# Side work of ScalarE and VectorE in the head rounds of a two-layer transformer block, put in another order

## The chip, the cores and the metric

The kernel runs on one core of a Trainium2 chip. The time is the device time of one execution in microseconds. TensorE (PE) multiplies, VectorE (DVE), ScalarE (ACT) and GpSimd (POOL) work on rows of 128 partitions, SyncE (SP) issues most transfers. Each engine takes its instructions in the order in which they are written; the engines wait for each other through semaphores.

## The reference

Two layers over 256 context and 256 latent tokens (512 columns here, feature on the partitions): feed-forward half, token mixer, feed-forward half. The head rounds are the gated delta rule of the token mixer, eight heads of width 128, in both directions:

```python
def _dn_inputs(p, dn_conv):
    y = jax.nn.silu(_dwconv(p[6], dn_conv))            # three taps over time
    q, k, v = [t.reshape(B, T, DN_HEADS, DN_DIM) for t in jnp.split(y, 3, axis=-1)]
    return (_l2norm(q), _l2norm(k), v) + ...

def _gated_delta_chunked(q, k, v, g, beta, s0):
    ...
    decay_mat = jnp.where(incl, jnp.exp(jnp.where(incl, diff, 0.0)), 0.0)
    a_mat = jnp.where(strict, einsum(kb, kc) * decay_mat, 0.0)
    sol = lax.linalg.triangular_solve(a_mat, rhs, left_side=True, lower=True, unit_diagonal=True)
    attn_intra = einsum(qc, kc) * decay_mat
    def step(s, inp):
        v_new = u_i - w_i @ s
        o = (q_i * exp(g_i)) @ s + a_i @ v_new
        s = s * exp(g_last) + (k_i * exp(g_last - g_i)) ^T @ v_new
```

Its output is normed, gated with silu of a fourth projection, and goes on to the branch products. In layer 1 only the 256 latent columns of q, the gate and the output are wanted.

## The kernel before

**Weights.** All weight matrices come as one stream of panels of 128 x 1024, four to a block B. A panel goes through `raw` (four slots), is split by ScalarE into a high part `whi` (`split`, L479, counted by `hi_ready`) and by VectorE into the low part `wlo` (`split`, L976, waits for `hi_ready`, counted by `lo_ready`), and TensorE multiplies it in 24 matmuls (L1569), 8 tiles by three products. SP loads the next panel into a slot when its low part is made.

**Head rounds.** `heads(l)` walks over the eight heads of a layer: the first head is prepared, then come seven rounds that finish head b - 1 and prepare head b (`head(l, b, True)`; six of them a loop, the seventh written out), and a last one that only finishes (`head(l, DNH, False)`). A round works on the panels of block B (panels 2 and 3) and of block B + 1 (panels 0 and 1) between its own products, so that TensorE has matmuls while others work. I write (B,3) for panel 3 of block B. A following round goes:

1. *Half levels.* The inverse of the triangular matrix is built in seven levels v for two directions d; half level h = 2v + d runs from 0 to 13. TensorE does eight 128x128 products (L1804, L1806) and then three panel matmuls. Its result is copied by ScalarE (L727, "copy h") and masked by VectorE (L1278, "mask h"); both are read by half level h + 2. The copies of half levels 12 and 13 are L730, the subtractions L1293 of VectorE stand in the place of masks. Panel (B,2) fills the half levels 0 to 7, (B,3) those from 8 on. Behind half level 11 and behind half level 13 stands a square sum of TensorE (L1889).
2. *Rest of the inverse*, L1830 to L1303.
3. *Scan*, four steps s over chunks: TensorE L1847, L1857, L1865, L1875, L1877, VectorE L1310, L1316, L1320, L1329 and L1332 between them.
4. *Front and output* (`output_and_front`): output norm of head b - 1 (L696, L1250, L487, L489, L1261, L1267, L712) and the first matrices of head b (L1759, L1253, `low_a` L1230, L1778, `first_level` L1236 and L1239).

**Side work.** Between the copies ScalarE does, for head b: bias `prep_in` (L626), first tap `prep_tap` (L639), request of the gathered decay rows `load_rows` (L644, an own transfer), `prep_silu` (L655, and L659 the squares), for head b - 1 the gate's Silu (L743, with a table load), and its halves of four splits. Between the masks VectorE does the other two taps `prep_conv` (L1178, L1180), its halves of the splits, and `decay` (L1211 and four L1216), which needs the gathered rows. A tap of VectorE waits for the tap of ScalarE, a split of VectorE for that of ScalarE; everything behind it in VectorE's queue waits too. The place of each piece of side work is written by hand, as conditions on (v, d).

## Time and profile before

| | us |
|---|---|
| median of 3 runs | 3571.32 |
| lowest, highest | 3563.38, 3581.49 |
| the profiled execution | 3567.69 |
| its span, first to last instruction | 3565.9 |
| TensorE busy | 3297.0 (92%) |
| VectorE busy | 1736.1 (49%) |
| ScalarE busy | 1418.2 (40%) |

The head rounds are 548 to 1047 us and 2535 to 3008 us of the span. The profile page gives busy time by engine and the chain that ended last. The windows view gives the busy time of each engine in stretches, and the granted TensorE clock as a share of full speed: 1.00 is 2.4 GHz, 0.50 is 1.2 GHz. The timeline has one row per instruction or run of alike ones, in brackets the idle time of the engine before it and what ended it.

### The profile page before, as it was taken

The numbers are of one execution on the slowest core, as the hardware profiler recorded it, in microseconds if no ns is written. First come the engines' busy times: TensorE is split into PE (matmuls) and PEld (weight loads), VectorE is DVE, ScalarE is ACT, GpSimd is POOL, SyncE is SP. The second block draws the span as 40 slices with busy tenths as digits, with TensorE's granted clock in tenths as the row PEclk, the third lists the DMA queues.
The fourth block names the chain that finished last, engine by engine and source line by source line (L and its number), as shares of the span: only waits on it lengthen the run. The fifth ranks groups of instructions, "written<-read, shape, count | busy, mean of one in ns | idle before, by whom it ended". The sixth has DMA issues, their size and how long they took to land.

```text
span 3565.9 us, 51673 instructions
## 1 busy us (share of the span) xinstructions
PE 3297.0 (92%) x18878; PEld 2729.3 (77%) x18878; DVE 1736.1 (49%) x3152; ACT 1418.2 (40%) x2197; POOL 131.5 (4%) x126
## 2 busy tenths in 40 slices
PE   5999989999989899999999999999798888999898
PEld 3778767777768667877788877777687777789898
DVE  2333346666643753434333433334566665666555
ACT  3222244545433642224322342223454544564544
POOL 0000001001000000000000000000000000000000
PEclk7999979998999999999999999998899989999999
DMA  6444421111112124222423243442111111324454
GB/s 227 159 142 141 153 77 43 46 35 48 40 40 90 42 72 148 94 89 96 165 95 100 100 153 136 154 146 95 54 47 41 47 42 52 120 96 166 152 183 148
DMA packets 101117, 363.43 MB, mean 102 GB/s; under 512 B 11136, under 2 KB 12672, under 8 KB 100864
## 3 DMA queue, kind: packets, MB, share of 16 engines
q1 hardware_dynamic: 98240, 353.00, 29.2%
q10 hardware_dynamic: 2752, 8.72, 0.7%
q8 instruction: 84, 1.38, 0.2%
q14 instruction: 41, 0.34, 0.0%
HBM read 360.56 MB, written 1.11 MB: 101 GB/s over the span
## 4 chain that ended last, share of the span: by engine, by line
PE 79%; DVE 9%; ACT 6%; issue 4%; DMA 1%; POOL 0%; DVEq 0%; SPq 0%; ACTq 0%; POOLq 0%
PE bank L1569 62%; PE bank L1804 2%; PE bank L1806 2%; ACT whi L479 2%; DVE wlo L976 2%; PE bank L1594 2%; PE bank L1857 1%; DVE scr_r L1278 1%; PE bank L1889 1%; PE bank L1700 1%; PE bank L1830 1%; ACT scr L896 1%; DVE h L1043 1%; PE bank L2000 1%; DVE scr L1320 1%
## 5 line engine op out<-in xcount | busy, mean ns | idle before, releaser
L1569 PE MATMUL bank<-uh,whi 128*128 128x512 f32 (+1 forms) x3008 | 1125.3, 374 | 46.3 <-ACTq L854 15.0
L1569 PE MATMUL bank<-ul,whi 128*128 128x512 f32 (+1 forms) x3008 | 1092.5, 363 | 0.0
L1569 PE MATMUL bank<-uh,wlo 128*128 128x512 f32 (+1 forms) x3008 | 1091.0, 363 | 0.5 <-DVE scr L1320 0.3
L976 DVE TENSOR_TENSOR wlo<-raw,whi 128x1024 fp32r<-128x1024 f32 x520 | 642.5, 1236 | 877.9 <-ACT whi L479 876.1
L479 ACT ACTIVATE whi<-raw 128x1024 fp32r<-128x1024 f32 x520 | 547.6, 1055 | 1224.4 <-PE bank L1569 1224.0
L1569 PEld LDWEIGHTS bank<-uh,whi 128*128 128x128 f32 x3008 | 584.1, 194 | 149.0 <-issue 56.3
L1569 PEld LDWEIGHTS bank<-uh,wlo 128*128 128x128 f32 x3008 | 582.9, 194 | 83.5 <-DVE scr L1320 1.8
L1569 PEld LDWEIGHTS bank<-ul,whi 128*128 128x128 f32 x3008 | 584.3, 194 | 70.4 <-issue 1.7
L1569 PE MATMUL bank<-bh,whi 128*128 128x512 f32 (+1 forms) x1088 | 387.9, 357 | 1.1 <-DVE h L1043 0.8
L1569 PE MATMUL bank<-bl,whi 128*128 128x512 f32 (+1 forms) x1088 | 384.5, 353 | 0.0
L1569 PE MATMUL bank<-bh,wlo 128*128 128x512 f32 (+1 forms) x1088 | 384.4, 353 | 0.0
L1569 PEld LDWEIGHTS bank<-bh,whi 128*128 128x128 f32 x1088 | 205.8, 189 | 33.5 <-issue 4.3
L1804 PEld LDWEIGHTS bank<-scr_r 128*128 128x128 f32 x896 | 142.5, 209 | 113.6 <-issue 73.8
L1569 PEld LDWEIGHTS bank<-bl,whi 128*128 128x128 f32 x1088 | 205.8, 189 | 28.7 <-issue 1.0
L1569 PEld LDWEIGHTS bank<-bh,wlo 128*128 128x128 f32 x1088 | 205.8, 189 | 28.4
L1804 PE MATMUL bank<-scr_r 128*128 128x128 f32 x896 | 154.0, 298 | 63.2 <-DVE scr_r L1278 63.2
L1079 DVE TENSOR_TENSOR scr<-scr,bank 128x512 f32<-128x512 f32 (+1 forms) x88 | 54.6, 620 | 256.9 <-PE bank L1569 256.5
L727 ACT ACTIVATE scr_r<-bank 128x512 fp32r<-128x512 f32 x192 | 114.5, 596 | 131.8 <-PE bank L1806 130.2
L1806 PE MATMUL bank<-scr_r 128*128 128x128 f32 x896 | 151.0, 295 | 0.0
L1278 DVE TENSOR_TENSOR scr_r<-bank,cst 128x512 fp32r<-128x512 f32 x192 | 128.5, 685 | 43.3 <-PE bank L1806 43.3
L440 POOL TENSOR_TENSOR scr<-scr 128x512 f32<-128x512 f32 (+1 forms) x42 | 47.4, 1129 | 2375.2 <-ACT scr L513 2374.2
L1806 PEld LDWEIGHTS bank<-scr_r 128*128 128x128 f32 x896 | 132.3, 212 | 0.0
(231 smaller groups left out, 3149.0 us busy)
## 6 DMA issues: line engine op xcount, KB each, us to landing
raw<-stream SPq DMA_DIRECT2D x520, 512.0 KB, 3.3
ada_raw<-stream SPq DMA_DIRECT2D x132, 512.0 KB, 5.2
gc_row<-gc_rows ACTq DMA_DIRECT2D x16, 512.0 KB, 3.7
m<-stream SPq DMA_DIRECT2D x8, 512.0 KB, 11.5
scr<-stream SPq DMA_DIRECT2D x4, 512.0 KB, 13.1
h<-h_in SPq DMA_DIRECT2D x1, 2048.0 KB, 17.6
cst<-consts SPq DMA_DIRECT2D x1, 1282.0 KB, 5.6
out<-m SPq DMA_DIRECT2D x8, 128.0 KB, 1.8
```

The source lines that it names most:

```text
L440: pool.tensor_tensor(nacc[:, c0:T], nacc[:, c0:T], nsq[:, t % 2, c0:T], ALU.add).then_inc(sq_added, 1)
L479: act.activation(whi[:, j, :], raw[:, j, :], ACT.Copy).then_inc(hi_ready, 1)
L727: act.activation(XT[:, d, :], bank[4 + d][:, :], ACT.Copy).then_inc(E["qtr_ready"], 1)
L896: last = act.activation(Pb[:, n % 2, a, q * w:(q + 1) * w], bank[2 + 2 * (n % 2) + a][:, q * w:(q + 1) * w], ACT.Exp, scale=HD ** -0.5, bi ...
L976: dve.tensor_tensor(wlo[:, j, :], raw[:, j, :], whi[:, j, :].bitcast(f32), ALU.subtract).then_inc(lo_ready, 1)
L1043: last = stt(out=h[:, t, a:b], in0=bank[j][:, a:b], scalar=hgate[:, t, k:k + 1], in1=h[:, t, a:b], op0=ALU.mult, op1=ALU.add)
L1079: dve.tensor_tensor(hbuf[:, k, c0:T], sil[:, k, c0:T], bank[2 * k + 1][:, c0:T], ALU.mult).then_inc(pair_done[k], 1)
L1278: dve.tensor_tensor(c4d(Pm[:, d, :]), c4d(bank[7 - d][:, :]), mask, ALU.mult).then_inc(E["pm_ready"], 1)
L1569: last = mm(bank[j][:, c0:T], w(t, a), x[:, t, c0:T], start=n == 0, stop=n == 3 * kts - 1)
L1594: last = mm(bank[4][at:at + 32, 0:256], cstat[:, 2 * j + kk, :], w[:, 512 * kk + 256 * half:512 * kk + 256 * half + 256], start=j == 0, st ...
L1804: mm(qt[:, sl(c)], Pm[:, d, sl(c)], x[:, d, sl(c)], start=v == 0 and c == 0, stop=False, skip_group_check=True)
L1806: last = mm(q[:, sl(c)], x[:, d, sl(c)], Pm[:, d, sl(c)], start=v == 0 and c == 0, stop=False, skip_group_check=True)
```

## The change

The side work in the head rounds is put in another order. No instruction is added or removed.

- ScalarE: gate Silu from behind copy 5 to behind copy 6, `prep_silu(0)` from 6 to 7, first half of split (B+1,0) from 7 to 8, `prep_silu(1)` from 8 to 10, split (B+1,1) from 10 to 11, split (B+1,2) from behind `prep_silu(2)` to behind the copy of half level 12. The third bias and tap stay behind copy 9.
- VectorE: `prep_conv(1)` from behind mask 4 to 5, split (B,3) from 3 to 6, `decay(0)` from behind the two L1293 to behind mask 8, split (B+1,0) from 6 to 9, `prep_conv(2)` from 8 to 11, split (B+1,1) from 9 to between the two L1293, `decay(1)` from scan step 0 to behind the two L1293, split (B+1,2) from scan step 1 into `output_and_front`: ahead of the first `first_level`, and in a last round between the two output products.

The core of the diff:

```diff
@@ scalar, head()
-                        if (v, d) == (2, 1):
+                        if at == 6:
                             have(act, E["head_ready"], o)
                             act.activation(gate[:, c0:T], gpre[:, c0:T], ACT.Silu)
-                        if follow and (v, d) == (3, 0):
+                        if follow and at == 7:
                             prep_silu(l, b, 0)
-                        if (v, d) == (3, 1):
+                        if at == 8:
                             split(B + 1, 0)
-                        if follow and (v, d) == (4, 0):
-                            prep_silu(l, b, 1)
-                        if follow and (v, d) == (4, 1):
+                        if follow and at == 9:
                             prep_in(l, b, 2)
                             prep_tap(l, b, 2)
-                        if (v, d) == (5, 0):
+                        if follow and at == 10:
+                            prep_silu(l, b, 1)
+                        if at == 11:
                             split(B + 1, 1)
+                        if at == 12:
+                            split(B + 1, 2)
                 if follow:
                     prep_silu(l, b, 2)
-                split(B + 1, 2)
@@ vector, output_and_front()
                     low_a(1)
+                    if output:
+                        split(P[("head", l)][0] + b + 1, 2)
                     first_level(0)
...
+                elif output:
+                    split(P[("head", l)][0] + b + 1, 2)
@@ vector, head()
-                        if (v, d) == (2, 1):
+                        if follow and at == 5:
+                            prep_conv(l, b, 1)
+                        if at == 6:
                             split(B, 3)
-                        if follow and (v, d) == (3, 0):
-                            prep_conv(l, b, 1)
-                        if (v, d) == (4, 0):
+                        if follow and at == 8:
+                            decay(l, b, 0)
+                        if at == 9:
                             split(B + 1, 0)
-                        if follow and (v, d) == (5, 0):
+                        if follow and at == 11:
                             prep_conv(l, b, 2)
-                        if (v, d) == (5, 1):
-                            split(B + 1, 1)
...
+                    if d == 0:
+                        split(B + 1, 1)
                 if follow:
-                    decay(l, b, 0)
+                    decay(l, b, 1)
...
-                    if follow and s == 0:
-                        decay(l, b, 1)
...
-                    if s == 1:
-                        split(B + 1, 2)
```

**VectorE in the half levels** of the seventh round of layer 0 (written out in the code), from masks 0 to 2 on. L1278 is a mask, L976 a split, L1178 and L1180 a pair of taps. Before:

```order
404 L1278 TENSOR_TENSOR scr_r<-bank,cst 128x512 [waits q_sum] x3
405 L1178 SCALAR_TENSOR_TENSOR kraw<-scr,hv,kraw 128x512 [waits tap_ready,hv_ready]
406 L1180 SCALAR_TENSOR_TENSOR kraw<-scr,hv,kraw 128x512 [waits dve_step]
407 L1278 TENSOR_TENSOR scr_r<-bank,cst 128x512 [waits q_sum]
408 L976 TENSOR_TENSOR wlo<-raw,whi 128x1024 [waits hi_ready]
409 L1278 TENSOR_TENSOR scr_r<-bank,cst 128x512 [waits q_sum]
410 L1178 SCALAR_TENSOR_TENSOR scr<-scr,hv 128x512 [waits tap_ready,hv_ready]
411 L1180 SCALAR_TENSOR_TENSOR scr<-scr,hv 128x512 [waits dve_step]
412 L1278 TENSOR_TENSOR scr_r<-bank,cst 128x512 [waits q_sum] x2
413 L976 TENSOR_TENSOR wlo<-raw,whi 128x1024 [waits hi_ready]
```

After (the mask is L1284, the taps L1180 and L1182, the split L978, the decay L1213 and L1218):

```order
404 L1284 TENSOR_TENSOR scr_r<-bank,cst 128x512 [waits q_sum] x3
405 L1180 SCALAR_TENSOR_TENSOR kraw<-scr,hv,kraw 128x512 [waits tap_ready,hv_ready]
406 L1182 SCALAR_TENSOR_TENSOR kraw<-scr,hv,kraw 128x512 [waits dve_step]
407 L1284 TENSOR_TENSOR scr_r<-bank,cst 128x512 [waits q_sum] x3
408 L1180 SCALAR_TENSOR_TENSOR scr<-scr,hv 128x512 [waits tap_ready,hv_ready]
409 L1182 SCALAR_TENSOR_TENSOR scr<-scr,hv 128x512 [waits dve_step]
410 L1284 TENSOR_TENSOR scr_r<-bank,cst 128x512 [waits q_sum]
411 L978 TENSOR_TENSOR wlo<-raw,whi 128x1024 [waits hi_ready]
412 L1284 TENSOR_TENSOR scr_r<-bank,cst 128x512 [waits q_sum] x2
413 L1213 COPY hgc<-tab 128x8 [waits dm_ready]
414 L1218 SCALAR_TENSOR_TENSOR m<-gc_row,hgc,cst 128x128 [waits it_ready,gcr_loaded,hgc_ready]
415 L1218 SCALAR_TENSOR_TENSOR m<-gc_row,hgc,cst 128x128 x3
```

The split of (B,3) moved from behind mask 3 to behind mask 6, the second pair of taps from behind mask 4 to behind mask 5, and the first decay came in behind mask 8.

**ScalarE in the half levels** of the same round, from its half of split (B,3) on. L727 is a copy, L479 a split, L743 the gate, L655 and L659 Silu and squares, L626 and L639 bias and tap. Before:

```order
313 L479 ACTIVATE whi<-raw 128x1024 [waits panel_done,raw_in3]
314 L727 ACTIVATE scr_r<-bank 128x512 [waits q_sum]
315 L743 ACT_TABLE_LOAD
316 L743 ACTIVATE scr<-gate_pre 128x512 [waits head_ready]
317 L727 ACTIVATE scr_r<-bank 128x512 [waits q_sum]
318 L655 ACTIVATE kraw<-kraw 128x512 [waits conv_ready]
319 L659 ACTIVATE scr<-kraw 128x512 [waits it_ready,silu_ready]
320 L727 ACTIVATE scr_r<-bank 128x512 [waits q_sum]
321 L479 ACTIVATE whi<-raw 128x1024 [waits panel_done,raw_in0]
322 L727 ACTIVATE scr_r<-bank 128x512 [waits q_sum]
323 L655 ACTIVATE scr<-scr 128x512 [waits conv_ready]
324 L659 ACTIVATE scr<-scr 128x512 [waits it_ready,silu_ready]
```

After (the gate is L744):

```order
313 L479 ACTIVATE whi<-raw 128x1024 [waits panel_done,raw_in3]
314 L727 ACTIVATE scr_r<-bank 128x512 [waits q_sum] x2
315 L744 ACT_TABLE_LOAD
316 L744 ACTIVATE scr<-gate_pre 128x512 [waits head_ready]
317 L727 ACTIVATE scr_r<-bank 128x512 [waits q_sum]
318 L655 ACTIVATE kraw<-kraw 128x512 [waits conv_ready]
319 L659 ACTIVATE scr<-kraw 128x512 [waits it_ready,silu_ready]
320 L727 ACTIVATE scr_r<-bank 128x512 [waits q_sum]
321 L479 ACTIVATE whi<-raw 128x1024 [waits panel_done,raw_in0]
322 L727 ACTIVATE scr_r<-bank 128x512 [waits q_sum]
323 L626 ACTIVATE scr<-bank,hv 128x2x256 [waits panel_done,hv_ready]
324 L639 ACTIVATE scr<-scr,hv 128x512 [waits pre_ready]
```

The split of (B,3) stays where it was; everything from the gate on stands one copy later, and the third bias and tap come ahead of the second Silu.

**VectorE in the scan** of the same round, steps 0 and 1. Before:

```order
431 L1320 TENSOR_SCALAR scr<-bank,hb 128x128 x2
432 L1216 SCALAR_TENSOR_TENSOR m<-gc_row,hgc,cst 128x128 x4
433 L1329 COPY scr<-bank 128x128 [waits ds_sum] x2
434 L1310 SCALAR_TENSOR_TENSOR scr<-bank,hb,scr 128x128 [waits ks_sum] x2
435 L1316 TENSOR_SCALAR scr<-bank,hb 128x128 [waits y_sum] x2
436 L1320 TENSOR_SCALAR scr<-bank,hb 128x128 x2
437 L1332 SCALAR_TENSOR_TENSOR scr<-scr,hb,bank 128x128 [waits s_ready,ds_sum] x2
438 L976 TENSOR_TENSOR wlo<-raw,whi 128x1024 [waits hi_ready]
439 L1310 SCALAR_TENSOR_TENSOR scr<-bank,hb,scr 128x128 [waits ks_sum] x2
```

After:

```order
432 L1329 TENSOR_SCALAR scr<-bank,hb 128x128 x2
433 L1336 COPY scr<-bank 128x128 [waits ds_sum] x2
434 L1319 SCALAR_TENSOR_TENSOR scr<-bank,hb,scr 128x128 [waits ks_sum] x2
435 L1325 TENSOR_SCALAR scr<-bank,hb 128x128 [waits y_sum] x2
436 L1329 TENSOR_SCALAR scr<-bank,hb 128x128 x2
437 L1339 SCALAR_TENSOR_TENSOR scr<-scr,hb,bank 128x128 [waits s_ready,ds_sum] x2
438 L1319 SCALAR_TENSOR_TENSOR scr<-bank,hb,scr 128x128 [waits ks_sum] x2
```

The four instructions of the second decay left step 0 and the split left step 1.

## Rows read from the trace of the kernel before

**Rows 1.** Page, the chain that ended last

```profile
PE 79%; DVE 9%; ACT 6%; issue 4%; DMA 1%; POOL 0%; DVEq 0%; SPq 0%; ACTq 0%; POOLq 0%
```

**Rows 2.** Windows: half levels, rests of layer 0, of layer 1; last round

```profile
sum 210.50, PE 185.37 PEld 152.28 DVE 122.81 ACT 132.19 POOL 43.09; mean PE 26.48 PEld 21.75 DVE 17.54 ACT 18.88 POOL 6.16
...
sum 232.80, PE 223.93 PEld 184.34 DVE 166.66 ACT 92.69 POOL 0.00; mean PE 31.99 PEld 26.33 DVE 23.81 ACT 13.24 POOL 0.00
...
sum 203.80, PE 172.72 PEld 152.00 DVE 110.49 ACT 121.28 POOL 21.07; mean PE 24.67 PEld 21.71 DVE 15.78 ACT 17.33 POOL 3.01
...
sum 212.90, PE 192.59 PEld 165.98 DVE 160.24 ACT 81.04 POOL 0.00; mean PE 27.51 PEld 23.71 DVE 22.89 ACT 11.58 POOL 0.00
...
991.80:1017.00 25.20, 21.73 (x147) 18.94 (x145) 12.44 (x17) 13.16 (x19) 6.27 (x5) 1.00 0.19 61
```

**Rows 3.** Timeline (start, us, operation), round at 738.4: masks, taps, splits

```profile
742.65 0.69 DVE L1278 TENSOR_TENSOR scr_r<-bank,cst 128x512 fp32r<-128x512 f32 x1 [0.89 <-PE bank L1806]
...
744.13 1.66 DVE L1180 SCALAR_TENSOR_TENSOR kraw<-scr,hv,kraw 128x512 f32<-128x512 f32 x1
...
744.78 0.56 PE L1804 MATMUL bank<-scr_r 128*128 128x128 f32 x4
...
747.40 1.23 DVE L976 TENSOR_TENSOR wlo<-raw,whi 128x1024 fp32r<-128x1024 f32 x1 [1.01 <-ACT whi L479]
...
759.18 0.75 DVE L1178 SCALAR_TENSOR_TENSOR scr<-scr,hv 128x512 f32<-128x512 f32 x1 [2.64 <-ACT scr L639]
```

**Rows 4.** Timeline, a square sum of TensorE, and ScalarE in the round at 738.4

```profile
707.02 1.02 PE L1889 MATMUL bank<-scr,cst 128*128 128x512 f32 x2
...
746.31 1.05 ACT L479 ACTIVATE whi<-raw 128x1024 fp32r<-128x1024 f32 x1
...
748.28 1.28 ACT L743 ACT_TABLE_LOAD   x1
...
751.64 0.63 ACT L659 ACTIVATE scr<-kraw 128x512 f32<-128x512 f32 x1
752.55 0.60 ACT L727 ACTIVATE scr_r<-bank 128x512 fp32r<-128x512 f32 x1 [0.27 <-PE bank L1806]
...
758.43 0.72 ACT L639 ACTIVATE scr<-scr,hv 128x512 f32<-128x512 f32 x1
```

**Rows 5.** Waits of the seven layer 0 rounds (waited for, us, times, longest)

```profile
PE bank L1804 <- DVE scr_r L1278: 25.1, 26, 1.9
DVE wlo L976 <- ACT whi L479: 25.1, 15, 3.1
```

**Rows 6.** Windows: length, busy by engine (PE, PEld, DVE, ACT, POOL), clock

```profile
759.10:762.50 3.40, 1.47 (x11) 1.05 (x10) 3.28 (x5) 1.48 (x3) 0.00 (x0) 0.99 0.00 0
762.50:765.90 3.40, 3.40 (x9) 2.08 (x9) 1.15 (x2) 0.60 (x1) 0.00 (x0) 0.50 0.49 154
776.00:786.00 10.00, 9.37 (x64) 7.92 (x62) 8.04 (x27) 2.67 (x5) 0.00 (x0) 1.00 0.15 52
```

**Rows 7.** Timeline, scan: weight loads in layer 0 and 1, a decay of VectorE

```profile
715.93 0.52 PEld L1847 LDWEIGHTS bank<-scr 128*128 128x128 f32 x4 [0.84 <-DVE scr L1329]
...
2753.36 0.52 PEld L1847 LDWEIGHTS bank<-scr 128*128 128x128 f32 x4 [1.06 <-DVE scr L1329]
...
2757.91 0.55 PEld L1857 LDWEIGHTS bank<-scr,xtf 128*128 128x128 f32 x4 [0.99 <-DVE scr L1310]
...
2751.97 1.13 DVE L1216 SCALAR_TENSOR_TENSOR m<-gc_row,hgc,cst 128x128 f32<-128x128 f32 x4
```

**Rows 8.** Timeline, front: first transposed level of VectorE, layer 0 and 1

```profile
734.49 0.69 DVE L1236 TENSOR_TENSOR lmat<-bank,cst 128x512 f32<-128x512 f32 x1 [2.08 <-PE bank L1778]
...
2769.80 0.69 DVE L1236 TENSOR_TENSOR lmat<-bank,cst 128x512 f32<-128x512 f32 x1 [0.96 <-PE bank L1778]
```

**Rows 9.** Timeline, TensorE behind the last round of layer 0

```profile
1046.88 0.79 PE L1569 MATMUL bank<-uh,whi 128*128 128x512 f32 x1 [8.47 <-ACTq L854]
```

**Rows 10.** Gathered decay rows: transfer from issue to landing

```profile
DMA to landing us min/median/max: 3.4/3.7/4.3
```

More of the change, by code:

```diff
@@ L730, in head @@
                             act.activation(X[:, d, :], bank[7 - d][:, :], ACT.Copy, scale=-1.0).then_inc(E["x_ready"], 1)
-                        if follow and (v, d) == (0, 1):
+                        at = 2 * v + d
+                        if follow and at == 1:
                             prep_in(l, b, 0)
                             prep_tap(l, b, 0)
-                        if follow and (v, d) == (1, 0):
+                        if follow and at == 2:
                             prep_in(l, b, 1)
-                        if follow and (v, d) == (1, 1):
+                        if follow and at == 3:
                             load_rows(l, b)
                             prep_tap(l, b, 1)
-                        if (v, d) == (2, 0):
+                        if at == 4:
                             split(B, 3)
-                        if (v, d) == (2, 1):
+                        if at == 6:
                             have(act, E["head_ready"], o)
                             act.activation(gate[:, c0:T], gpre[:, c0:T], ACT.Silu)
-                        if follow and (v, d) == (3, 0):
+                        if follow and at == 7:
                             prep_silu(l, b, 0)
-                        if (v, d) == (3, 1):
+                        if at == 8:
                             split(B + 1, 0)
-                        if follow and (v, d) == (4, 0):
-                            prep_silu(l, b, 1)
-                        if follow and (v, d) == (4, 1):
+                        if follow and at == 9:
                             prep_in(l, b, 2)
                             prep_tap(l, b, 2)
-                        if (v, d) == (5, 0):
+                        if follow and at == 10:
+                            prep_silu(l, b, 1)
+                        if at == 11:
                             split(B + 1, 1)
+                        if at == 12:
+                            split(B + 1, 2)
                 if follow:
                     prep_silu(l, b, 2)
-                split(B + 1, 2)
                 log_exp()
@@ L1278, in head @@
                         dve.tensor_tensor(c4d(Pm[:, d, :]), c4d(bank[7 - d][:, :]), mask, ALU.mult).then_inc(E["pm_ready"], 1)
-                        if follow and (v, d) == (2, 0):
+                        at = 2 * (v - 1) + d
+                        if follow and at == 2:
                             prep_conv(l, b, 0)
-                        if (v, d) == (2, 1):
+                        if follow and at == 5:
+                            prep_conv(l, b, 1)
+                        if at == 6:
                             split(B, 3)
-                        if follow and (v, d) == (3, 0):
-                            prep_conv(l, b, 1)
-                        if (v, d) == (4, 0):
+                        if follow and at == 8:
+                            decay(l, b, 0)
+                        if at == 9:
                             split(B + 1, 0)
-                        if follow and (v, d) == (5, 0):
+                        if follow and at == 11:
                             prep_conv(l, b, 2)
-                        if (v, d) == (5, 1):
-                            split(B + 1, 1)
                 for d in range(2):
```

## The prediction, with its working

> **What bounds the kernel now.** I read the page first: the chain that ended last is TensorE for 79% of the span [rows 1], so time goes where TensorE stands still. The diff touches only the head rounds, so next come the windows of those rounds. There are 16: seven of layer 0 that also prepare the next head (the "following" rounds), seven of layer 1, and one last round in each layer. I cut each round at the start of its half level 13, the last of the fourteen half levels; a half level is one level of the inversion for one direction, with three panel matmuls behind it. The sum rows say: 210.5 us in the seven stretches of half levels of layer 0 (30.07 a round) and 232.8 us in their rests (33.26), 203.8 us (29.11) and 212.9 us (30.41) in layer 1, and 25.2 us of half levels in a last round [rows 2].
>
> Then one round as VectorE sees it. The masks of half levels 1 and 2 come 0.89 + 0.69 = 1.58 us apart, each released by TensorE: an undisturbed half level costs 1.59 us. The mask of half level 2 ends at 742.65 + 0.69 = 743.34, and the level that reads it (half level 4) starts at 744.78 without having waited. So a mask or a copy may be 1.44 us late before TensorE stands still. This spare is the number on which all of this rests [rows 3].
>
> What exceeds it? Thirteen intervals of 1.59 us and the square sum of 1.02 us that stands between levels 11 and 12 [rows 4] make 21.7 us, against the 30.07 measured. VectorE's split of (B,3), queued behind mask 3, stands 1.01 us until ScalarE's half of it is done, since ScalarE makes that half only behind its copy 4; mask 4, the next in VectorE's queue, cannot start before 747.40 + 1.23 less the overlap of 0.1, while level 4, begun at 744.78, releases it 1.05 us later (level 2 began two half levels before level 4, at 741.60, and released mask 2 at 742.65). It is 2.7 us late. The same at splits (B+1,0) and (B+1,1), and at the third tap, which VectorE takes at half level 8 while ScalarE's part comes behind copy 9 (2.64 us of idle) [rows 3]. In the seven layer 0 rounds VectorE waits 25.1 us for ScalarE's halves of splits, and TensorE 25.1 us for masks, visibly; more of its wait lies in the weight loads [rows 5]. ScalarE is no better off: its next copy depends on a level that waits for the late mask.
>
> The rest of the 30.07 is clock. In the round that begins at 738.4 TensorE is busy 1.47 of 3.40 us just before 762.5, and in the next 3.4 us the granted clock is 0.50, the lower level of 1.2 GHz [rows 6]. Stepping through the old order at the higher level with the durations of [rows 3, 4] I get 27.0 us for a round of layer 0 and 25.9 for one of layer 1; the missing 3.1 and 3.2 us are the slow stretches, and the mutual waits themselves are 27.0 - 21.7 = 5.3 us. All of them lie behind the sparse half levels 5 to 11, hardly any in the rests.
>
> **The change, part by part.** *The half levels.* No instruction is added or taken away; each VectorE step now stands at least one half level behind its ScalarE part. I step through the new order from the start of level 0, release of half level h at 1.06 + 1.59h, with copy 0.60, mask 0.69, bias and tap 0.7 each, ScalarE split 1.05, table load 1.28, Silu and square 0.63 each, VectorE split 1.22, tap pair 1.5 [rows 3, 4] and decay 1.13 [rows 7] with 0.3 for the small copy ahead of it.
> ScalarE, layer 0: on time through copy 6; the table load and Silu behind it make copy 7 0.8 us late; then 0.95 (copy 8), 0.9 (9), 1.1 (10, behind the third bias and tap), 1.25 (11, behind the second Silu and square). All are under 1.44.
> VectorE, layer 0: mask 3 is 1.4 us late as before (the second tap instruction takes 1.66 us beside GpSimd [rows 3]), about at the limit and costing 0.1; afterwards never over 0.6 us. The split of (B,3) behind mask 6 ends at 12.9 us, and TensorE wants that panel behind level 8, at 13.6.
> So layer 0 gives 13 x 1.59 + 1.02 + 0.1 = 21.8 us; gain 30.07 - 21.8 = 8.3, times 7: 58 us.
> Layer 1: from half level 8 the panels are half as wide, TensorE asks faster and ScalarE becomes the bound there: copy 8 at 14.5 us, split, copy, bias and tap, copy, Silu and square (0.85 at half width), copy 11 at 19.2, level 13 at 20.2. Gain 8.9, times 7: 62 us.
> Last rounds have no taps and no square sum: 25.2 becomes 13 x 1.59 = 20.7; twice 4.5: 9 us.
>
> *The scan.* The second decay leaves it. TensorE's weight load for the second step stood 0.84 us (layer 0) and 1.06 us (layer 1) behind VectorE's state copy, which had the decay ahead of it; I take 0.75 and 0.9, since a panel matmul still stands between. The split of panel 2 leaves it too: the wait of 0.99 us in layer 1 falls to the 0.3 or so of its neighbours; in layer 0 output products cover all but 0.1 [rows 7]. Against this, in layer 1 the second decay now ends some 0.3 us after the product behind it is ready. Together 0.85 x 7 + 1.3 x 7 = 15 us.
>
> *The front.* The split (1.22 us) now stands ahead of the first transposed level. VectorE idled 2.08 us there in layer 0 and 0.96 in layer 1 [rows 8]: nothing, and 0.3 us of delay that the next level, four us away, does not see. Without that cover it would be 1.22 x 14 = 17 us.
>
> *The end of the last rounds.* There the split stands between the two output products, in a chain that nothing covers; TensorE waits 8.47 us at its end [rows 9]. Cost 1.22 less 0.3 gained in the scan: twice 0.9, 2 us.
>
> *Decay 0 at half level 8.* It needs the gathered rows, which ScalarE requests at 6.3 us; landing takes 3.4 to 4.3 us [rows 10], so they are there at 10.6 and VectorE comes at 14.4. Nothing.
>
> **Sum**: 58 + 62 + 9 + 15 - 2 = 142 us. The profiled execution took 3567.7 us (span 3565.9 and 1.8 around it), 3.6 under the median of 3571.3. So 3425.7 on its scale, 3429 on the median's.
>
> **The clock, weighed.** The gain holds 14 x 3.15 = 44 us of slow clock which I expect to go with the sparse half levels. The row for it: from 776 to 786 in the scan TensorE is busy 9.37 of 10 us in short pieces that wait for VectorE again and again, and the granted clock is 1.00 (2.4 GHz) [rows 6]; the half levels of the last round, with 4.5 us of waits in them, also stand at 1.00 [rows 2]. The Trainium skill, "TensorE: Matmul & The Clock Gate", section "A second HAM failure mode: psum-queue depth-cycling", says that frequent small idles between groups of matmuls are enough to make the clock swing. By that rule the slow stretches would stay and the time would be near 3473; by the scan's row they go. I follow the row, since the scan is made just as that section describes.
>
> **Rivals.**
> A: the slow stretches stay, in the half levels or moved into scan and front. For: all rounds but the last ones have them now, and 1.02 us square sums and short waits remain. Against: the scan's row. 3429 + 44 = 3473. Chance 0.17.
> B: ScalarE becomes the bound in the half levels. It is busy 132.19 / 7 = 18.9 us in those of layer 0 [rows 2]; with the split that moves in that is 19.9 of 21.8. Copies 10 and 11 have 0.2 to 0.3 us of spare left; a copy that is 0.5 us later from half level 7 on costs as much on each later half level that ScalarE bounds, 1 to 2 us a round. At 2 us: 28 us, 3457. Chance 0.14.
> C: the waits go elsewhere whole (a panel not ready behind level 8, where 0.7 us is left, in every round, or a buffer that frees later), so that the change doesn't do what it says. About 3560. Chance 0.04.
> D, slower: the denser rounds fall to 1.2 GHz in scan and front as well. Going by the two levels, 10 us at the lower clock cost 3.7 us in half levels with idle time and up to 5 where TensorE is never idle, as in the rests (busy 223.9 of 232.8). It needs more than 142 / 14 = 10 us a round, over 20 us of slow clock in a round of some 54; at 25 us the time is 3600. No row shows a slow rest longer than a few us. Chance 0.01.
>
> **How the numbers follow.** The forecast holds 0.64: 3429, its own range 3412 to 3447 (1.2 us a round either way from the stepping). B reaches to 3457 and A to 3473; to leave out no more than 2 in 10 the range is 3408 to 3475. 0.5% of this time is 18 us, about what a measurement of this kernel can tell from no change. Faster by more: forecast, A and B, 0.95; within: C, 0.04; slower 0.01.
>
> **What would show it.** Half levels: masks 1.59 us apart all through, fourteen of them in some 21.8 and 20.2 us; no wait of VectorE's split for ScalarE; granted clock 1.00 in the windows of all rounds; rests of about 32.4 and 29.1 us. The scan's state copy follows its product at once. Wrong would be: copies of ScalarE over 1.4 us late behind the Silus (B), clock 0.50 in scan or front (A, D), TensorE waiting behind level 8 for the low half of panel 3 (C), or a last round that ends more than 1 us later.

## The result, and the profile after

The changed kernel takes 3422.5 us (median of 4 runs, 3419.5 to 3424.6) against 3571.9 for the kernel before in the same comparison: ratio 0.958, 95% interval 0.9555 to 0.9606. The forecast was 3429, the range 3408 to 3475. The profiled execution took 3423.6 us with a span of 3421.8; before it was 3567.7 and 3565.9, so 144.1 us are to be found in the trace.

The page of the changed kernel, its share of the chain that ended last:

```profile
span 3421.8 us, 51673 instructions
PE 84%; DVE 7%; ACT 4%; issue 3%; DMA 1%; POOL 0%; SPq 0%; DVEq 0%; ACTq 0%; POOLq 0%
```

The same instructions as before, with TensorE now 84% of the chain instead of 79% [rows 1]. The windows of the changed kernel, cut like [rows 2]: the seven half-level stretches of layer 0, their rests, the half levels of layer 1, their rests (length first, then busy time by engine).

```profile
sum 153.37, PE 153.37 PEld 135.96 DVE 123.63 ACT 128.97 POOL 43.16; mean PE 21.91 PEld 19.42 DVE 17.66 ACT 18.42 POOL 6.17
...
sum 226.33, PE 221.88 PEld 184.28 DVE 166.22 ACT 91.71 POOL 0.00; mean PE 31.70 PEld 26.33 DVE 23.75 ACT 13.10 POOL 0.00
...
sum 141.82, PE 141.82 PEld 129.62 DVE 107.67 ACT 115.73 POOL 21.08; mean PE 20.26 PEld 18.52 DVE 15.38 ACT 16.53 POOL 3.01
...
sum 200.98, PE 191.98 PEld 166.41 DVE 161.36 ACT 81.68 POOL 0.00; mean PE 27.43 PEld 23.77 DVE 23.05 ACT 11.67 POOL 0.00
...
927.40:948.25 20.85, 20.85 (x146) 19.11 (x145) 11.52 (x17) 12.99 (x20) 6.27 (x5) 1.00 0.16 51
```

The last line is the half levels of the last round of layer 0. TensorE is now busy for the whole of the half levels (153.37 of 153.37), where it was busy 185.37 of 210.50. Per following round, and with the forecast beside it:

| us | before | forecast | after |
|---|---|---|---|
| half levels, layer 0 | 30.07 | 21.8 | 21.91 |
| rest, layer 0 | 33.26 | 32.4 | 32.33 |
| half levels, layer 1 | 29.11 | 20.2 | 20.26 |
| rest, layer 1 | 30.41 | 29.1 | 28.71 |
| half levels, last rounds | 25.2 | 20.7 | 20.85 |

Times seven, seven and two, that is 57 + 62 + 9 us in the half levels and 6 + 12 in the rests, 146 us, 2 more than the span fell. Those 2 us were given back outside these stretches, mostly between the head rounds of the two layers, where the program is unchanged: that part took 1488.5 us before and 1491.4 in this execution.

Next VectorE's timeline in the round that begins at 710.3, the one that answers to [rows 3] (masks L1284, taps L1180 and L1182, split L978, decay L1218):

```profile
720.11 0.74 DVE L1180 SCALAR_TENSOR_TENSOR scr<-scr,hv 128x512 f32<-128x512 f32 x1
720.89 0.75 DVE L1182 SCALAR_TENSOR_TENSOR scr<-scr,hv 128x512 f32<-128x512 f32 x1
721.56 0.69 DVE L1284 TENSOR_TENSOR scr_r<-bank,cst 128x512 fp32r<-128x512 f32 x1
722.16 1.22 DVE L978 TENSOR_TENSOR wlo<-raw,whi 128x1024 fp32r<-128x1024 f32 x1
723.29 0.69 DVE L1284 TENSOR_TENSOR scr_r<-bank,cst 128x512 fp32r<-128x512 f32 x1
724.26 0.69 DVE L1284 TENSOR_TENSOR scr_r<-bank,cst 128x512 fp32r<-128x512 f32 x1 [0.28 <-PE bank L1811]
```

The splits and the taps show no bracket: whatever VectorE takes is there. The decay behind mask 8 waits 0.21 us, for VectorE's own small copy ahead of it. Where a mask waits, it waits for TensorE. ScalarE runs the other way, without idle time from the gate's table load on:

```profile
721.71 1.28 ACT L744 ACT_TABLE_LOAD   x1
723.01 0.63 ACT L744 ACTIVATE scr<-gate_pre 128x512 f32<-128x512 f32 x1
723.54 0.58 ACT L727 ACTIVATE scr_r<-bank 128x512 fp32r<-128x512 f32 x1
...
728.47 0.58 ACT L727 ACTIVATE scr_r<-bank 128x512 fp32r<-128x512 f32 x1
...
730.13 0.58 ACT L727 ACTIVATE scr_r<-bank 128x512 fp32r<-128x512 f32 x1
```

Mask 8 shows the release of half level 8, 724.26; counting half levels of 1.59 us from it, copy 7 is 0.9 us late, copy 10 (728.47) 1.0 and copy 11 (730.13) 1.1. The stepping had 0.8, 1.1 and 1.25, all under the spare of 1.44. In layer 1 ScalarE's copies follow its side work without idle time from the gate on, and TensorE's weight loads wait for them a little, as in the round that begins at 2616.0:

```profile
2634.35 0.19 PEld L1809 LDWEIGHTS bank<-scr_r 128*128 128x128 f32 x1 [0.24 <-ACT scr_r L727]
```

There ScalarE is the bound, as forecast; its copy 11 starts 19.0 us after the start of level 0, where 19.2 was stepped.

Third, the granted clock: four windows of the changed kernel, half levels of one round of each layer, a rest of layer 0 and the rest of the seventh round of layer 1.

```profile
569.42:601.80 32.38, 31.75 (x196) 26.36 (x196) 23.82 (x58) 13.15 (x22) 0.00 (x0) 1.00 0.10 34
710.30:732.25 21.95, 21.95 (x148) 19.41 (x147) 17.83 (x35) 18.53 (x30) 7.19 (x5) 1.00 0.20 72
...
2781.97:2813.10 31.13, 29.87 (x181) 25.66 (x180) 23.39 (x59) 11.78 (x23) 0.00 (x0) 0.95 0.11 35
2789.30:2792.70 3.40, 3.40 (x14) 3.07 (x14) 1.90 (x8) 1.97 (x5) 0.00 (x0) 0.51 0.00 0
```

All fourteen half-level stretches and all rests but this one stand at 1.00, 2.4 GHz; in this one 3.4 us are at the lower level. One rest of layer 1 was like that before, too (31.0 us, granted clock 0.94).

### The profile page after: what moved, and what is told of

Its sections match the earlier page's. It is cut to its first block, busy times and chain, and to the rows that moved or that the text cites. A ratio compares the mean times of both kernels' runs of the same rounds, so it can differ in the third digit from the quotient of the medians.

```text
span 3421.8 us, 51673 instructions
## 1 busy us (share of the span) xinstructions
PE 3229.0 (94%) x18878; PEld 2692.4 (79%) x18878; DVE 1735.3 (51%) x3152; ACT 1409.0 (41%) x2197; POOL 131.6 (4%) x126
## 4 chain that ended last, share of the span: by engine, by line
PE 84%; DVE 7%; ACT 4%; issue 3%; DMA 1%; POOL 0%; SPq 0%; DVEq 0%; ACTq 0%; POOLq 0%
PE bank L1574 66%; PE bank L1811 3%; PE bank L1809 2%; DVE wlo L978 2%; PE bank L1599 2%; ACT whi L479 1%; PE bank L1862 1%; PE bank L1705 1%; ACT scr L898 1%; PE bank L1870 1%; DVE h L1045 1%; PE bank L1880 1%; PE bank L1882 1%; PE bank L2005 1%; PE bank L2028 1%
## 5 line engine op out<-in xcount | busy, mean ns | idle before, releaser
L479 ACT ACTIVATE whi<-raw 128x1024 fp32r<-128x1024 f32 x520 | 547.8, 1055 | 1224.7 <-PE bank L1574 1224.3
L978 DVE TENSOR_TENSOR wlo<-raw,whi 128x1024 fp32r<-128x1024 f32 x520 | 642.3, 1235 | 807.0 <-ACT whi L479 805.2
L1284 DVE TENSOR_TENSOR scr_r<-bank,cst 128x512 fp32r<-128x512 f32 x192 | 131.1, 688 | 71.6 <-PE bank L1811 71.6
L1809 PEld LDWEIGHTS bank<-scr_r 128*128 128x128 f32 x896 | 131.5, 189 | 25.7 <-issue 5.0
L727 ACT ACTIVATE scr_r<-bank 128x512 fp32r<-128x512 f32 x192 | 113.4, 590 | 69.6 <-PE bank L1811 68.3
L1811 PE MATMUL bank<-scr_r 128*128 128x128 f32 x896 | 136.6, 275 | 0.0
L1809 PE MATMUL bank<-scr_r 128*128 128x128 f32 x896 | 131.5, 269 | 0.0
L1811 PEld LDWEIGHTS bank<-scr_r 128*128 128x128 f32 x896 | 118.0, 192 | 0.0
```

The lines of the kernel that those rows point to most:

```text
L479: act.activation(whi[:, j, :], raw[:, j, :], ACT.Copy).then_inc(hi_ready, 1)
L727: act.activation(XT[:, d, :], bank[4 + d][:, :], ACT.Copy).then_inc(E["qtr_ready"], 1)
L978: dve.tensor_tensor(wlo[:, j, :], raw[:, j, :], whi[:, j, :].bitcast(f32), ALU.subtract).then_inc(lo_ready, 1)
L1284: dve.tensor_tensor(c4d(Pm[:, d, :]), c4d(bank[7 - d][:, :]), mask, ALU.mult).then_inc(E["pm_ready"], 1)
L1809: mm(qt[:, sl(c)], Pm[:, d, sl(c)], x[:, d, sl(c)], start=v == 0 and c == 0, stop=False, skip_group_check=True)
L1811: last = mm(q[:, sl(c)], x[:, d, sl(c)], Pm[:, d, sl(c)], start=v == 0 and c == 0, stop=False, skip_group_check=True)
```

## The experiments

### Which engine's order matters

Two kernels, each with one engine's order old and the other's new. `dve_alone` is the changed kernel with ScalarE's old order:

```diff
@@ scalar, head(), against the changed kernel
-                        if at == 6:
+                        if (v, d) == (2, 1):
                             have(act, E["head_ready"], o)
...
-                        if at == 8:
+                        if (v, d) == (3, 1):
                             split(B + 1, 0)
...
-                        if at == 11:
+                        if (v, d) == (5, 0):
                             split(B + 1, 1)
-                        if at == 12:
-                            split(B + 1, 2)
                 if follow:
                     prep_silu(l, b, 2)
+                split(B + 1, 2)
```

> The changed kernel with ScalarE's order in the half levels put back to that of the kernel before; VectorE keeps the new order. Theory (what counts is that VectorE takes a piece a half level behind ScalarE's part; ScalarE's own shifts only spread its load): stepping gives 21.7 us of half levels a following round in layer 0 and 20.0 in layer 1, as in the changed kernel (21.9 and 20.3), so 3422, within 5 us. Rival (both reorderings are needed, since ScalarE's copies come late behind the early gate): each following round 1 to 2 us longer, 3436 to 3450.

Measured: 3421.5 us (3420.0 to 3424.0), ratio to before 0.9577, interval 0.955 to 0.9603. Half levels of the seven rounds of layer 0, then of layer 1:

```profile
sum 153.46, PE 153.44 PEld 135.95 DVE 123.60 ACT 128.07 POOL 43.19; mean PE 21.92 PEld 19.42 DVE 17.66 ACT 18.30 POOL 6.17
...
sum 141.57, PE 141.57 PEld 129.55 DVE 107.38 ACT 117.47 POOL 20.98; mean PE 20.22 PEld 18.51 DVE 15.34 ACT 16.78 POOL 3.00
```

21.92 and 20.22 us a round: the changed kernel's times. ScalarE's part of the diff brings nothing that can be measured; the rival falls.

`act_alone` is the kernel before with ScalarE's new order (the diff above turned round and put on the kernel before).

> The kernel before with ScalarE's new order; VectorE keeps the old one. Theory: each mutual wait grows, since ScalarE's part comes later still while VectorE stands for it: stepping at the full clock gives 31.1 us (layer 0) and 30.4 (layer 1) of half levels against 27.0 and 25.9, and 28.0 in a last round against 25.1, so 3571 + 7 x 4.1 + 7 x 4.5 + 6 = 3637 with the slow clock as it is, up to 20 more if it grows. Rival (ScalarE's order by itself takes part of the gain): under 3571.

Measured: 3659.8 us (3654.3 to 3666.1), ratio 1.0247, interval 1.0215 to 1.0279: slower than before by 90 us, 23 more than the stepping at unchanged clock gave. The half levels of layer 0 summed, the rests of layer 1 summed, and one of these rests:

```profile
sum 234.35, PE 196.78 PEld 160.31 DVE 122.88 ACT 131.90 POOL 43.17; mean PE 28.11 PEld 22.90 DVE 17.55 ACT 18.84 POOL 6.17
...
sum 228.96, PE 209.72 PEld 183.19 DVE 161.62 ACT 80.68 POOL 0.00; mean PE 29.96 PEld 26.17 DVE 23.09 ACT 11.53 POOL 0.00
...
2669.52:2703.80 34.28, 31.82 (x180) 28.48 (x179) 23.56 (x63) 11.58 (x22) 0.00 (x0) 0.80 0.05 20
```

The half levels of the following rounds are not where the 23 us lie: they grew by 24 us in layer 0 (33.5 us a round) and 32 in layer 1, 55 in all, where 60 were stepped. What the stepping had no term for are slow stretches elsewhere. The rests of layer 1 took 16 us more than before (212.9 to 229.0), six of the seven with a granted clock of 0.80 to 0.95, and the half levels of the two last rounds took 32.9 and 33.5 us instead of 25.1, 16 us more where 6 were stepped. Delaying ScalarE's part while VectorE stands at the old place makes every wait longer. So what the change does is in VectorE's order; ScalarE's reordering alone costs 2.5%.

### What one wait costs, and what four cost

`one_wait` puts one of VectorE's pieces back:

```diff
@@ vector, head(), against the changed kernel
-                        if at == 6:
+                        if at == 3:
                             split(B, 3)
```

> The changed kernel with one of VectorE's pieces put back: the split of (B,3) stands behind mask 3 again, while ScalarE's half comes behind copy 4. Theory: one mutual wait of 1.4 us a round and no slow clock, since TensorE idles too little: 16 x 1.4 = 22 us, 3445, granted clock 1.00 in the half levels. Rival (any idle time brings the slow clock): 22 + up to 14 x 3.1 = 3488, with stretches at 0.50 in the half levels.

Measured: 3457.9 us (3449.2 to 3462.4), ratio 0.9674: 35 us over the changed kernel, between the two expectations. The windows say why. One round of layer 0, a round of layer 1, what lies ahead of its slow stretch, the slow stretch, and a later round of layer 1:

```profile
602.60:625.80 23.20, 22.23 (x148) 19.34 (x147) 17.93 (x35) 18.55 (x30) 7.18 (x5) 1.00 0.21 68
2478.70:2508.30 29.60, 28.37 (x148) 25.57 (x147) 15.98 (x32) 17.12 (x28) 0.00 (x0) 0.71 0.22 71
2486.60:2490.20 3.60, 2.37 (x17) 1.85 (x16) 2.53 (x4) 1.64 (x3) 0.00 (x0) 1.00 0.33 100
2490.20:2507.20 17.00, 17.00 (x70) 15.39 (x70) 8.69 (x16) 10.35 (x16) 0.00 (x0) 0.50 0.18 60
2647.50:2669.20 21.70, 20.46 (x147) 18.40 (x146) 15.24 (x34) 16.57 (x28) 3.50 (x5) 1.00 0.21 69
```

In twelve of the sixteen rounds the wait costs what was stepped, 1.3 to 1.5 us (23.2 against 21.9, 21.7 against 20.3), with the clock at 1.00. In four rounds (the last of layer 0 and the first three of layer 1) the same wait in the same place is followed by a slow stretch of 7 to 17 us at 1.2 GHz, and the round's half levels take up to 29.6. So one wait of 1.4 us can bring the clock down and mostly doesn't; the runs of this kernel also lie 13 us apart, where those of the changed kernel lie 5 apart. What picks the four rounds stays open.

`four_waits` puts four pieces a half level ahead of ScalarE's part:

```diff
@@ vector, head(), against the changed kernel
-                        if at == 6:
+                        if at == 3:
                             split(B, 3)
-                        if follow and at == 8:
-                            decay(l, b, 0)
-                        if at == 9:
+                        if at == 7:
                             split(B + 1, 0)
-                        if follow and at == 11:
+                        if follow and at == 8:
                             prep_conv(l, b, 2)
+                            decay(l, b, 0)
+                        if at == 10:
+                            split(B + 1, 1)
...
-                    if d == 0:
-                        split(B + 1, 1)
```

> The changed kernel with four of VectorE's pieces one half level ahead of ScalarE's part: split (B,3) behind mask 3, split (B+1,0) behind 7, the third taps and decay 0 behind 8, split (B+1,1) behind 10. Scan and front stay as changed. Stepping at the full clock: 27.8 and 27.5 us of half levels a following round, 24.8 in a last one: 6 x 7 + 7.2 x 7 + 4 x 2 = 100 us over the changed kernel, 3523. Theory on the clock (sparse half levels bring it down): a further 3 us a round, 44, so about 3565 with 0.50 in the windows of the half levels. Rival (the slow stretches had another cause): 3523 and 1.00 in all half levels.

Measured: 3565.1 us (3551.8 to 3568.1, 10 runs), ratio 0.9981, interval 0.9966 to 0.9996: the whole gain is gone again with scan and front left as changed. Its waits in layer 0 (waited for, us, times, longest), the granted clock over most of the head rounds of each layer, the half levels of layer 0 and of layer 1 summed, and those of a last round:

```profile
DVE wlo L978 <- ACT whi L479: 55.6, 22, 3.9
...
PE bank L1808 <- DVE scr_r L1284: 28.0, 21, 2.2
...
546.50:1000.00 453.50, 420.96 (x2469) 350.87 (x2468) 297.64 (x646) 229.62 (x360) 49.40 (x35) 0.93 0.13 43
2490.00:2900.00 410.00, 361.75 (x2149) 316.49 (x2149) 261.68 (x634) 199.22 (x348) 23.82 (x34) 0.86 0.14 45
...
sum 213.20, PE 186.32 PEld 155.10 DVE 132.12 ACT 130.77 POOL 43.13; mean PE 26.62 PEld 22.16 DVE 18.87 ACT 18.68 POOL 6.16
...
sum 220.60, PE 190.65 PEld 167.97 DVE 119.43 ACT 121.91 POOL 20.98; mean PE 27.24 PEld 24.00 DVE 17.06 ACT 17.42 POOL 3.00
...
985.92:1010.72 24.80, 21.56 (x146) 18.77 (x144) 11.93 (x17) 13.99 (x20) 6.27 (x5) 1.00 0.13 43
```

3523 was stepped at the higher level, 3565 with the clock. The clock is back at 0.93 and 0.86, and the total is what the theory said. That it fits to the microsecond is partly luck: the half levels take 30.5 and 31.5 us a round, so over the stepped 27.8 and 27.5 the slow clock costs 2.7 us in layer 0 and 4.0 in layer 1, where 3 was taken for both. The last round is worth a look: it has no taps, so three of the four waits stand in it; it takes the stepped 24.8 us, and its clock stays at 1.00. In `one_wait` the same round, with one of these waits, has a slow stretch. So the amount of waiting alone does not say whether the clock falls.

### The clock by itself

The two above change waits and clock together. `idle_filled` keeps the waits between VectorE and ScalarE of the kernel before and takes away TensorE's idleness:

```diff
@@ tensor, head(), against the kernel before
+                def filler(h):
+                    n = {5: 5, 6: 2, 8: 6, 10: 8}.get(h, 0) if follow else 0
+                    if n:
+                        pe.wait_ge(E["pre_ready"], 3 * (l * DNH + b) + 1)
+                    for _ in range(n):
+                        mm(bank[1][:, :], nidr[:, :], bc(idr[:, :], TC, 128), start=True, stop=True)
...
                     project(fill)
+                    filler(2 * v)
...
                     level(v, 1)
                     project(fill)
+                    filler(2 * v + 1)
```

> The kernel before, with TensorE given idle work where it waits: in following rounds 5, 2, 6 and 8 matmuls of 128x512 (0.23 us each at the higher clock) into a bank that nobody reads then, behind half levels 5, 6, 8 and 10. Its order of side work, and so its mutual waits, stay. Theory (the slow stretches come from the idle time in the sparse half levels, and cost 3.1 us a following round): the half levels of a following round fall from 30.1 and 29.1 us to 27.0 and 25.9 with granted clock 1.00, 44 us less: 3525. Rival (the slow clock has another cause, or its cost was really part of the waits): 3569 or more, since 21 matmuls of 0.23 us are added.

Measured: 3539.6 us (3539.0 to 3547.3), ratio 0.9915, interval 0.9891 to 0.9939. With 21 matmuls more a round, the kernel is 31 us faster. Half levels of layer 0 and of layer 1 summed, one round with its clock, VectorE's wait for ScalarE's splits in the seven rounds of layer 0, and the half levels of the last round of layer 0:

```profile
sum 191.56, PE 190.93 PEld 161.51 DVE 122.26 ACT 132.14 POOL 43.13; mean PE 27.28 PEld 23.07 DVE 17.47 ACT 18.88 POOL 6.16
...
sum 186.77, PE 179.56 PEld 154.98 DVE 109.12 ACT 121.37 POOL 20.98; mean PE 25.65 PEld 22.14 DVE 15.59 ACT 17.34 POOL 3.00
...
730.30:757.70 27.40, 27.33 (x170) 23.08 (x168) 17.35 (x30) 19.07 (x29) 7.19 (x5) 1.00 0.23 77
...
DVE wlo L976 <- ACT whi L479: 23.8, 14, 2.3
...
972.33:1000.85 28.52, 26.20 (x146) 23.17 (x145) 12.47 (x17) 13.08 (x19) 6.27 (x5) 0.82 0.16 53
```

27.4 and 26.7 us a round against 30.07 and 29.11 [rows 2], and 27.0 and 25.9 stepped, all fourteen with the clock at 1.00. VectorE waits for the splits as before (23.8 us against 25.1 [rows 5]). So 36 us of the 44 come back in the half levels. Whether the filling costs the other 8, or the stepping was that much too low, no run tells. The other step of the theory, that they then stay back, holds only in part: the rests of layer 1 grew from 212.9 to 215.8 us and the last round of layer 0, which was not filled, from 25.2 to 28.5, with a clock of 0.82 instead of 1.00. Slow stretches that are kept out of one sparse place appear in part in the next.

### The scan

`scan_back` leaves the half levels as changed and puts VectorE's decay 1 and split of panel 2 back into the scan:

```diff
@@ vector, against the changed kernel
                     low_a(1)
-                    if output:
-                        split(P[("head", l)][0] + b + 1, 2)
                     first_level(0)
...
-                elif output:
-                    split(P[("head", l)][0] + b + 1, 2)
...
-                if follow:
-                    decay(l, b, 1)
...
+                    if follow and s == 0:
+                        decay(l, b, 1)
...
+                    if s == 1:
+                        split(B + 1, 2)
```

> The changed kernel with only the scan, the front and the end of the last rounds put back: decay 1 in scan step 0 and VectorE's split of panel 2 in step 1. Theory: rests become 33.3 and 30.1 us again instead of 32.3 and 28.3; 0.95 x 7 + 1.8 x 7 = 19, less 1 at the ends of the last rounds: 3422 + 18 = 3440, half levels 21.9 and 20.3 as in the changed kernel, clock 1.00. Rival (with dense half levels the scan's waits are covered): 3422 to 3426.

Measured: 3443.8 us (3443.2 to 3444.3), ratio 0.9641: 21 us over the changed kernel, 3 over the theory. Rests of layer 0 summed, rests of layer 1 summed, one rest of layer 1, and a piece of it:

```profile
sum 232.56, PE 223.74 PEld 184.22 DVE 165.35 ACT 92.37 POOL 0.00; mean PE 31.96 PEld 26.32 DVE 23.62 ACT 13.20 POOL 0.00
...
sum 216.02, PE 196.25 PEld 170.80 DVE 162.95 ACT 82.41 POOL 0.00; mean PE 28.04 PEld 24.40 DVE 23.28 ACT 11.77 POOL 0.00
...
2543.60:2574.50 30.90, 28.05 (x181) 24.64 (x180) 23.37 (x60) 11.79 (x23) 0.00 (x0) 0.94 0.10 36
2553.00:2556.40 3.40, 3.10 (x14) 3.00 (x15) 2.09 (x9) 1.60 (x4) 0.00 (x0) 0.51 0.00 0
```

Layer 0's rests are those of [rows 2] to 0.3 us. Layer 1's are 30.9 a round, where before they were 30.1 to 31.4 and mostly 30.1: the same scan now has a slow stretch of 3.4 us in it in five of the seven rounds, where behind the sparse half levels one of seven had it. In each of the five that is the extra 0.8 us, together the 3 us over the theory.

### How near ScalarE is to the bound

Rival B said that ScalarE's copies have 0.2 to 0.3 us of spare. `act_packed` adds nothing and takes two splits earlier:

```diff
@@ scalar, head(), against the changed kernel
                             prep_tap(l, b, 2)
+                        if at == 9:
+                            split(B + 1, 1)
                         if follow and at == 10:
                             prep_silu(l, b, 1)
-                        if at == 11:
-                            split(B + 1, 1)
-                        if at == 12:
+                        if at == 10:
                             split(B + 1, 2)
```

> The changed kernel with ScalarE's halves of split (B+1,1) and (B+1,2) taken earlier, behind copies 9 and 10 beside the third taps and the second Silu, so that nothing is added and copies 10 and 11 come later. Theory (a copy may be 1.44 us late, ScalarE has 0.2 to 0.3 us of that left there): stepping gives copy 11 3.2 us late in layer 0 and 3.4 in layer 1 and 0.85 and 1.6 us more of half levels a following round: 3422 + 6 + 11 = 3439. Rival (the spare of the copies is larger than stepped): 3422, within 4.

Measured: 3433.3 us (3431.7 to 3438.3), ratio 0.9613: 11 over the changed kernel. Its half levels in sum are 156.47 us in layer 0 (22.35 a round, +0.44 where +0.85 was stepped) and 150.38 in layer 1 (21.48, +1.22 where +1.6 was). The spare is real and nearly used up, and the stepping overstates what lies beyond it by about 0.4 us a round.

### A last round that ends sooner

`tail_and_tap`:

```diff
@@ vector, against the changed kernel
-                elif output:
-                    split(P[("head", l)][0] + b + 1, 2)
                 if output:
                     dve.wait_ge(E["eo_ready"], o + 1)
                     dve.tensor_tensor(gate[:, c0:T], gate[:, c0:T], eo[:, 0, c0:T], ALU.mult).then_inc(E["on_ready"], 1)
+                if output and not front:
+                    split(P[("head", l)][0] + b + 1, 2)
...
-                        if follow and at == 2:
+                        if follow and at == 3:
                             prep_conv(l, b, 0)
```

> The changed kernel with two edits: in the last rounds VectorE's split of panel 2 stands behind the second output product instead of ahead of it, and the first pair of taps stands behind mask 3 instead of mask 2. Theory: the end of a last round loses 1.1 us (twice: 2.2), and the 0.24 us that TensorE waits in half levels 4 and 5 of six layer 0 rounds go (1.5): 3422 - 3.7 = 3418.5, hardly to be told from 3422 in the time but plain in the windows. Rival: the split behind the product delays the next one, which the first panel of the branch needs: 3422 or more.

Measured: 3417.8 us (3415.2 to 3418.5, 5 runs), ratio to before 0.9566, interval 0.9547 to 0.9584. That overlaps with the changed kernel's interval, so only the trace can say what did it. From half level 13 of the last round to the branch's first panel TensorE takes 29.8 instead of 30.7 us in layer 0 and 26.9 instead of 27.6 in layer 1: 1.5 of the 2.2 expected. The taps gave nothing: the half levels of layer 0 sum to 153.37, as in the changed kernel. Its VectorE rows:

```profile
717.24 1.74 DVE L1180 SCALAR_TENSOR_TENSOR kraw<-scr,hv,kraw 128x512 f32<-128x512 f32 x1
719.02 0.75 DVE L1182 SCALAR_TENSOR_TENSOR kraw<-scr,hv,kraw 128x512 f32<-128x512 f32 x1
```

The first of the pair now takes 1.74 us instead of the second 1.66 [rows 3]: the delay beside GpSimd's work went along and reached half levels 6 and 7 instead of 5 and 6 (by the trace; the expectation counted 4 and 5). The remaining 3 us to the changed kernel's median are not the edit's: between the two profiled executions, 5.8 us apart, 2.5 us lie between the head rounds of the two layers and 1.3 behind the second, where both programs are alike, and 0.9 in the last full rest of layer 1, which has no slow stretch here.

## Why the prediction was right

**The spare of 1.44 us** was the step everything rested on, and it held: `one_wait` costs 1.3 to 1.5 us where one mutual wait comes back at the higher clock, the changed kernel's copies are up to 1.1 us late at no cost, and `act_packed`, which goes beyond the spare, pays.

**Half levels**: 21.8, 20.2 and 20.7 us were forecast, 21.91, 20.26 and 20.85 came. The 0.1 us more in layer 0 is the slow tap, which costs 0.2 where 0.1 was taken: the first round, which has no work of GpSimd beside the taps, takes 21.72 us, the others 21.90 to 21.95. It is VectorE's reordering that does it (`dve_alone`); the forecast had stepped both engines without saying which mattered.

**The clock**: 44 us of the 142 were put down to the slow stretches. `idle_filled` shows 36 of them in the half levels as an effect of TensorE's idleness, with the waits in place, and `four_waits` brings them back; the other 8 rest on the stepping alone. Rival A did not happen in the changed kernel, but its mechanism exists: `one_wait` keeps slow stretches in the half levels and `scan_back` has them in the scan. What decides whether a given wait is followed by one stays open. In its half levels the changed kernel has no such wait left; that its scan stayed clear of them was a near thing, and no row of before could have told. The weighing of the scan's row against the rule of the Trainium skill ("TensorE: Matmul & The Clock Gate", "A second HAM failure mode: psum-queue depth-cycling") came out for the row in 13 of 14 rests, as many as before. The forecast called the scan "made just as that section describes"; that section tells of bf16 matmuls of 512 columns, and the scan's are 128x128 in f32, so only the frequent small idles are alike. `scan_back` says how narrow that was: with 1.8 us more of waits in a rest of layer 1, the same scan falls to 1.2 GHz for 3.4 us in five of seven rounds, as the rule would have it. So the split and decay taken out of the scan belong to the reasons why the clock stayed up, which the forecast had not counted.

**Scan**: 15 us were forecast, 18 came (6.5 and 11.9). The term of layer 1 was mis-sized: 1.3 us a round taken, 1.7 measured. The weight load that stood 1.06 us behind the state copy [rows 7] no longer shows a wait, and the one that waited 0.99 us waits 0.30, as forecast:

```profile
2644.90 0.52 PEld L1852 LDWEIGHTS bank<-scr 128*128 128x128 f32 x4
...
2645.84 0.56 PEld L1862 LDWEIGHTS bank<-scr,xtf 128*128 128x128 f32 x4 [0.30 <-DVE scr L1319]
```

That is 1.06 + 0.69 = 1.75 us, what a rest without slow stretches fell by (30.1 to 28.3). So the first wait went whole, where 0.9 was taken, and the 0.3 us charged for the later decay ahead of the product was not paid.

**Front**: nothing was forecast for the split ahead of the first transposed level. VectorE's idle time there fell from 2.08 to 0.93 us in layer 0 and from 0.96 to none in layer 1 [rows 8], which is the cover being used:

```profile
758.43 1.22 DVE L978 TENSOR_TENSOR wlo<-raw,whi 128x1024 fp32r<-128x1024 f32 x1
760.58 0.69 DVE L1238 TENSOR_TENSOR lmat<-bank,cst 128x512 f32<-128x512 f32 x1 [0.93 <-PE bank L1783]
```

**End of the last rounds**: 2 us of loss were forecast, 0.9 each. Layer 0 lost 0.8 (29.9 to 30.7 us up to the branch's first panel), layer 1 gained 0.8 (28.4 to 27.6). The split costs the same 1.0 us at the end of both, where 1.22 was taken: TensorE's wait grew from 8.47 us [rows 9] to 9.48 in layer 0 and from 6.50 to 7.51 in layer 1. The rows are the one of layer 0 after, those of layer 1 before and after, and a piece of the last round of layer 1 before:

```profile
978.91 0.80 PE L1574 MATMUL bank<-uh,whi 128*128 128x512 f32 x1 [9.48 <-ACTq L856]
...
3005.64 0.58 PE L1569 MATMUL bank<-uh,whi 128*128 128x256 f32 x1 [6.50 <-ACTq L854]
...
2861.52 0.58 PE L1574 MATMUL bank<-uh,whi 128*128 128x256 f32 x1 [7.51 <-ACTq L856]
...
2991.40:2994.80 3.40, 3.21 (x13) 2.94 (x14) 1.54 (x6) 0.00 (x0) 0.00 (x0) 0.50 0.47 153
```

What the forecast missed is the gain ahead of that end in layer 1, 1.9 us instead of 0.3. It goes together with a slow stretch of 3.4 us that the scan of that round had before and no longer has; how the 1.9 us divide between it and the split's leaving, no run shows.

**The other rivals**: ScalarE's load in the half levels of layer 0, which B put at 19.9 us, measured 18.4 (128.97 / 7), since the split that moved in stands at the end of these stretches and runs behind it. Of C there is nothing in the trace: the gathered rows land in 3.4 to 4.2 us, and no panel is waited for behind level 8. Of D there is the one rest with 3.4 us at 1.2 GHz, where over 20 us a round would have been needed.

## What to carry to other kernels

Where two engines hand pieces to each other beside a chain that both serve, put the taker's instruction behind the giver's in time, not only in dependence: one step too early and the wait blocks everything behind it in its queue. Measure the spare of the chain first (the end of a mask to the start of the level that reads it) and count lateness against it; and charge a sparse stretch of TensorE with more than its idle time. Moving the giver later without the taker makes it worse, so such edits go in pairs, or the taker's alone.

## What the runs showed of the hardware that was not expected

- Adding 21 idle matmuls a round made a kernel 31 us faster (3570.6 to 3539.6), by keeping TensorE at 2.4 GHz through its waits.
- The same wait of 1.4 us, in the same place of sixteen like rounds, brought the clock to 1.2 GHz in four of them and not in twelve.
- A scan that ran at 2.4 GHz in six of seven layer 1 rounds behind sparse half levels, which had a slow stretch of their own, has 3.4 us at 1.2 GHz in five of the seven behind dense ones (`scan_back`).
- The last round of layer 0 with three waits (24.8 us, TensorE busy for 21.6 of them) kept 2.4 GHz in `four_waits`, and the same round with one of them did not in `one_wait`.
- A tap of VectorE beside GpSimd's L454 took 1.66 to 1.74 us instead of 0.75, whichever of the pair stood there; in the first round of layer 0, without GpSimd's work, both take 0.74 to 0.75. The masks, which read one operand from a bank, took 0.68 us beside it as elsewhere. The two L454 of GpSimd took 3.46 us with the taps behind mask 2 and 2.52 with them behind mask 3.
